# Order of VectorE's and ScalarE's work beside the projections of a first block: retention heads four pieces later, one square for eight exponentials

## The reference, cut to what matters

```python
xn = rms_norm(h, norm_in_g)
proj = xn @ w_in                       # 1024 x 6144
q, k, v, g_ret, x_lru, g_lru = split(proj)
q, k = rotary(q), rotary(k) * 128 ** -0.5          # 8 heads of 128
o_ret = group_norm_heads(chunkwise_retention(q, k, v))
y_ret = o_ret * silu(g_ret)

xc = causal_depthwise_conv(x_lru, conv_w, conv_b)
r = sigmoid(block_diag(xc, gate_a)); i = sigmoid(block_diag(xc, gate_x))
log_a = -8 * r * softplus(-lru_lambda)
a = exp(log_a)
mult = sqrt(max(1 - exp(2 * log_a), 0))
b = mult * (i * xc)
o_lru[t] = a[t] * o_lru[t - 1] + b[t]              # a scan over the tokens
y_lru = o_lru * silu(g_lru)
h = h + concat(y_ret, y_lru) @ w_out
```

## Time and profile before

| | us |
|---|---|
| median of 3 runs | 1706.65 (1706.38 to 1706.9) |
| the profiled execution | 1706.55 |
| its span | 1704.8 |
| TensorE busy | 1670.0 |
| VectorE busy | 1256.5 |
| ScalarE busy | 842.9 |

### The profile page before, as it was taken

The page is one execution under the profiler, slowest core; times in us unless marked ns, Lnnn a source line. Parts: engine busy times, 40 slices in busy tenths (PEclk is TensorE's granted clock), DMA queues, the critical chain, the costliest instruction groups (busy, mean ns, idle before and its releaser), DMA issues.

```text
span 1704.8 us, 25221 instructions
## 1 busy us (share of the span) xinstructions
PE 1670.0 (98%) x9808; PEld 1426.1 (84%) x9808; DVE 1256.5 (74%) x2205; ACT 842.9 (49%) x1370; POOL 0.2 (0%) x4
## 2 busy tenths in 40 slices
PE   9989999999999999999999999999999999999998
PEld 9888888777787778888888888889778989979997
DVE  7999777875778798856877775347756786678874
ACT  6665555554324443347444442336553455466653
POOL 0000000000000000000000000000000000000000
PEclk9999999999999999999999999999999999999999
DMA  8646543232234335533545556324322444547653
GB/s 340 228 161 236 193 152 108 67 123 62 69 111 161 121 133 186 206 128 99 141 149 188 191 196 222 99 75 139 101 83 64 134 147 152 172 156 169 196 198 124
DMA packets 79078, 254.91 MB, mean 150 GB/s; under 512 B 14320, under 2 KB 18672, under 8 KB 78320
## 3 DMA queue, kind: packets, MB, share of 16 engines
q1 hardware_dynamic: 73488, 244.91, 43.8%
q10 hardware_dynamic: 5472, 8.39, 1.5%
HBM read 252.19 MB, written 1.07 MB: 149 GB/s over the span
## 4 chain that ended last, share of the span: by engine, by line
PE 78%; DVE 13%; ACT 5%; issue 3%; DMA 0%; ACTq 0%; DVEq 0%
PE bank L725 66%; DVE w_lo L1830 3%; PE bank L868 2%; PE bank L1037 2%; PE bank L1023 2%; PE bank L1115 2%; PE bank L1014 2%; ACT w_hi L1225 1%; DVE mod_w L1887 1%; PE bank L1104 1%; DVE probT L1887 1%; DVE att L2460 1%; DVE xc L1930 1%; DVE resid_x L2326 0%; DVE bank L2458 0%
## 5 line engine op out<-in xcount | busy, mean ns | idle before, releaser
L1830 DVE TENSOR_TENSOR w_lo<-w_raw,w_hi 128x1024 fp32r<-128x1024 f32 (+1 forms) x356 | 426.9, 1210 | 253.5 <-ACT w_hi L1225 251.9
L1225 ACT ACTIVATE w_hi<-w_raw 128x1024 fp32r<-128x1024 f32 (+1 forms) x356 | 370.0, 1048 | 339.2 <-PE bank L725 284.5
L725 PE MATMUL bank<-hT_hi,w_hi 128*128 128x512 f32 (+1 forms) x1280 | 446.0, 348 | 1.7 <-ACT zo L1555 0.6
L725 PE MATMUL bank<-hT_hi,w_lo 128*128 128x512 f32 (+1 forms) x1280 | 437.5, 342 | 0.0
L725 PE MATMUL bank<-hT_lo,w_hi 128*128 128x512 f32 (+1 forms) x1280 | 437.3, 342 | 0.0
L725 PEld LDWEIGHTS bank<-hT_hi,w_hi 128*128 128x128 f32 x1280 | 242.2, 189 | 30.4 <-issue 3.1
L725 PEld LDWEIGHTS bank<-hT_hi,w_lo 128*128 128x128 f32 x1280 | 242.1, 189 | 27.9
L725 PEld LDWEIGHTS bank<-hT_lo,w_hi 128*128 128x128 f32 x1280 | 242.4, 189 | 27.1 <-issue 1.0
L1887 DVE SCALAR_TENSOR_TENSOR mod_w<-mod_w,c_rows 128x1024 f32<-128x1024 f32 x96 | 117.0, 1218 | 8.4 <-DMA mod_w<-in_mod_weights 8.4
L725 PE MATMUL bank<-w_hi,hT_hi 128*128 128x512 f32 x272 | 114.7, 422 | 0.4 <-issue 0.4
L725 PE MATMUL bank<-w_lo,hT_hi 128*128 128x512 f32 x272 | 106.6, 392 | 0.0
(11 more groups left out here) (393 smaller groups left out, 2794.9 us busy)
## 6 DMA issues: line engine op xcount, KB each, us to landing
w_raw<-in_weights SPq DMA_DIRECT2D x356, 512.0 KB, 3.9
mod_w<-in_mod_weights SPq DMA_DIRECT2D x96, 512.0 KB, 4.1
nbias<-in_window_bias ACTq DMA_DIRECT2D x32, 128.0 KB, 3.2
resid_c<-in_ctx ACTq DMA_DIRECT2D x2, 1024.0 KB, 6.8
gain_mix<-gain_rows SPq DMA_DIRECT2D x3, 512.0 KB, 5.7
gain_ffn<-gain_rows SPq DMA_DIRECT2D x3, 512.0 KB, 4.2
c_rows<-in_conditions SPq DMA_DIRECT2D x1, 1024.0 KB, 5.6
gatew<-in_gate_weights SPq DMA_DIRECT2D x1, 1024.0 KB, 11.6
```

The costliest lines, as they stand in the source:

```text
L725: mm = pe.matmul(held[key][:, oc], st, mv_, start=(opens and k == 0 and t == 0 and i == 0), stop=(closes and k == tiles - 1 and t == 2), s ...
L1225: a.activation(w_hi[:, p % RING, :, used], w_raw[:, p % RING, :].rearrange("p (k n) -> p k n", k=KP)[:, :, used], ACT.Copy).then_inc(hi_re ...
L1830: v.tensor_tensor(w_lo[:, p % RING, :, used], w_raw[:, p % RING, :].rearrange("p (k n) -> p k n", k=KP)[:, :, used], w_hi[:, p % RING, :, ...
```

## The change

The early retention heads start after skipping 8 products' banks, four pieces later, behind pieces 25, 27, ... 35. ScalarE writes a = exp(log_a) in place, and then the square of all of it in one instruction, in place of exp(2 log_a) by eight. VectorE's product by the square root is two halves (`lru_drive`), each scan waits for VectorE's instruction before it, and the decays, statistics, scans, gatings and lo halves stand in a new order, with the halves of the pieces placed explicitly and `ahead` reduced by 2 at decays and statistics. One modulation block moves ahead of head 7's product. ScalarE's order of square roots, silus and hi halves changes likewise.

```diff
+EARLY_SKIP = 8
-            early = Beside(retention_early(), RET_EVERY, 0)
+            early = Beside(retention_early(), RET_EVERY, EARLY_SKIP)
...
-            def ret_sqrt(h):
-                ahead(("ro", h))
+            def ret_sqrt(h, split=True):
+                if split:
+                    ahead(("ro", h))
...
             act.wait_ge(*lam_scaled.at(0))
+            act.wait_ge(*A.last())
             for n in range(HEADS):
-                act.wait_ge(*lru_ix.at(n))
-                a.activation(xc[:, n, :], lru_r[:, n, :], ACT.Exp, scale=lam[:, 1, n:n + 1]).then_inc(*A.tell(lru_e2, n))
+                a.activation(lru_r[:, n, :], lru_r[:, n, :], ACT.Exp, scale=lam[:, 0, n:n + 1]).then_inc(*A.tell(lru_a, n))
                 if n % 4 == 3:
                     split_hi(23 + n // 4)
             act.wait_ge(*A.last())
+            act.wait_ge(*lru_ix.at(HEADS - 1))
+            a.activation(xc[:], lru_r[:], ACT.Square).then_inc(*A.tell(lru_e2, 0))
             tok(4, v1, ACT.Copy)
-            for n in range(HEADS):
-                a.activation(lru_r[:, n, :], lru_r[:, n, :], ACT.Exp, scale=lam[:, 0, n:n + 1]).then_inc(*A.tell(lru_a, n))
-                if n % 4 == 3:
-                    split_hi(25 + n // 4)
+            split_hi(26)
             act.wait_ge(*lru_clamped.at(0))
             a.activation(xc[:], xc[:], ACT.Sqrt, bias=1.0).then_inc(*A.tell(lru_mult, 0))
             tok(5, sg, ACT.Silu)
```

VectorE:

```diff
+            def lru_drive(n):
+                v.tensor_tensor(lru_i[:, n:n + 4, :], lru_i[:, n:n + 4, :], xc[:, n:n + 4, :], ALU.mult).then_inc(*W.next())
             def lru_scan(n):
+                dve.wait_ge(*W.last())
...
-            for n in range(4, HEADS):
+            for n in range(4, HEADS - 1):
                 lru_input(n)
             mod_ops(2)
+            lru_input(HEADS - 1)
             split_lo(23)
             mod_ops(2)
-            dve.wait_ge(*lru_e2.at(HEADS - 1))
+            dve.wait_ge(*lru_e2.at(0))
             v.tensor_scalar(xc[:], xc[:], 1.0, -1.0, ALU.min, ALU.mult).then_inc(*W.tell(lru_clamped, 0))
             split_lo(24)
             mod_ops(2)
             split_lo(25)
             mod_ops(2)
             split_lo(26)
```

More of the change, by code:

```diff
@@ L1346, in _ @@
             tok(5, sg, ACT.Silu)
-            ret_sqrt(0)
-            ret_sqrt(1)
+            split_hi(30)
+            silu_T(6)
+            split_hi(32)
+            ret_sqrt(0, False)
+            split_hi(34)
+            ret_sqrt(1, False)
             ret_mix(0)
-            silu_T(6)
-            ret_sqrt(2)
+            split_hi(36)
+            ret_sqrt(2, False)
             ret_mix(1)
-            split_hi(32)
+            silu_T(7)
             for n in range(4):
                 lru_mix(n)
-            ret_sqrt(3)
+            split_hi(37)
+            ret_sqrt(3, False)
             ret_mix(2)
-            silu_T(7)
-            ret_mix(3)
-            split_hi(36)
             for n in range(4, HEADS):
                 lru_mix(n)
+            ret_mix(3)
             act.dma_start(gout_row[:], gout_in).then_inc(gout_loaded, 16)
@@ L1933, in conv_pair, with ret_decay @@
                     W.mark(conv_ready, n)
-            def ret_decay(h):
+            def ret_decay(h, more=0):
                 key = ("rs", h)
-                ahead(key)
+                ahead(key, more)
                 dve.wait_ge(*filled_at(key))
@@ L1944, in ret_decay, with ret_stats @@
                 v.tensor_tensor(sT[:, h % 2, T:T + P], ps[:, T:T + P], decay[:, h, 0:P], ALU.mult).then_inc(*W.drain(key))
-            def ret_stats(h):
+            def ret_stats(h, more=0):
                 key = ("ro", h)
-                ahead(key)
+                ahead(key, more)
                 dve.wait_ge(*filled_at(key))
@@ L1961, in ret_norm, with ret_var_of @@
                 ret_normed(h)
-            def ret_var_of(h):
-                ret_stats(h)
+            def ret_var_of(h, more=0):
+                ret_stats(h, more)
                 v.tensor_scalar(bnst[:, 2 + h % 2, 0:2], att[:, 2 * (h % 2):2 * (h % 2) + 2, 1], EPS, None, ALU.add)\
@@ L2058, in _ @@
             split_lo(26)
-            dve.wait_ge(decay_loaded, 16)
[L2060 to L2066, removed]
-                lru_scan(n)
+            dve.wait_ge(*lru_mult.at(0))
+            lru_drive(0)
+            split_lo(27)
+            lru_drive(4)
+            split_lo(28)
@@ L2068, in _ @@
+            dve.wait_ge(decay_loaded, 16)
+            ret_decay(0, -2)
+            for n in range(4):
+                lru_scan(n)
+            split_lo(29)
+            ret_decay(1, -2)
+            ret_var_of(0, -2)
+            split_lo(30)
+            ret_normed(0)
             for g in range(2):
-                ahead((("in", 5), g))
                 dve.wait_ge(*drained_at((("in", 5), g)))
             ret_gate(0)
-            ret_decay(2)
-            lru_scan(3)
-            ret_norm(1)
+            for n in (4, 5):
+                lru_scan(n)
@@ L2075, in _ @@
+            split_lo(31)
+            ret_decay(2, -2)
+            ret_var_of(1, -2)
+            lru_scan(6)
+            ret_normed(1)
             ret_gate(1)
+            split_lo(32)
             ret_lo(0)
[L2077 to L2080, removed]
+            lru_scan(7)
+            dve.wait_ge(*W.last())
+            for n in range(4):
+                lru_gating(n)
+            ret_decay(3, -2)
+            split_lo(34)
+            ret_var_of(2, -2)
@@ L2081, in _ @@
+            ret_normed(2)
             ret_gate(2)
             ret_lo(1)
[L2083 to L2086, removed]
+            for n in range(4, HEADS):
+                lru_gating(n)
+            split_lo(35)
+            ret_var_of(3, -2)
             for n in range(4):
-                lru_gating(n)
-            ret_norm(3)
+                lru_lo(n)
+            ret_normed(3)
             ret_gate(3)
             ret_lo(2)
-            for n in range(4):
-                lru_lo(n)
@@ L2094, in _ @@
-            split_lo(35)
-            ret_lo(3)
             split_lo(36)
             for n in range(4, HEADS):
-                lru_gating(n)
-            for n in range(4, HEADS):
                 lru_lo(n)
+            ret_lo(3)
             mod_ops(2)
```

## The result

The changed kernel takes 1710.18 us (median of 16 runs, 1709.62 to 1712.07) against 1706.71 for the kernel before on the same chips (16 runs, 1706.28 to 1707.56): 3.47 us more, ratio 1.002, 95% interval 1.0013 to 1.0027. The forecast was 1709.5, its range 1704 to 1712.3, and the likeliest case a loss. The profiled execution took 1709.74 us, span 1708.0.

The account below looks back on a forecast made before the run. VectorE's arrival at the second q block's rotation was taken to pace TensorE and the end: new idle 6.6 plus scans and drive 1.0 less old idle 4.7 gives +2.9 (2.85 by the walk), 1709.5 us, range 1704 to 1712.3.

Parts of the forecast that it names:

- the end follows VectorE's arrival at the rotation: A delay of VectorE at the second q block's rotation (line 1911, at 140.36 before) delays the end.
- The Square: ScalarE's one Square of 128x2048, 1.91 us, ends at 85.51; VectorE waits 4.6 us for it at the clamp.
- the case with one: A table load before the Square adds 1.28 us; chance 0.05, within a rival of 0.15 for late roots and loads.
- The 3.6 us wait and the clock behind it: TensorE's wait before the first retention output (line 800) and its half-speed clock go when retention starts four pieces later.
- The stalls at pieces 31 and 35: TensorE waits for VectorE's late lo halves, 1.5 us at piece 31 and 2.0 us at piece 35.
- The walk: VectorE's queue priced step by step from head 7's product to the second q block's rotation, reached at 143.2, 2.85 us later.
- the wait at piece 39: TensorE, there at 144.9, waits 3.6 us for VectorE's lo half, done at 148.5.
- counted 0 for the clock: Slow TensorE clock behind new gaps at pieces 23 and 39 adds 0, bounds 0 and 0.5 us.
- The term for the scans: VectorE's eight scans, each waiting for the instruction before, step 0.71 instead of 0.60: 0.9 us, bounds 0 and 1.0.
- the main case: The forecast of VectorE late at the rotation: +2.85 us, own range +1.2 to +4.5, chance 0.55.
- the terms for the scores of head 1: TensorE gives scores 1 only behind piece 27, at 104.95, leaving VectorE idle 1.06 us.
- a gain: Rival: retention no longer stalls TensorE and the Square is no wait; -3.7 up to -7.5 us, say 1701.5; chance 0.13.

Follow-up runs that it names:

- Experiments 2: Changed kernel with VectorE's second modulation pair and the lo half of piece 23 ahead of the wait for the Square: 1707.79 us, 0.56 over the kernel before.
- experiment 6: Changed kernel with one modulation block moved from ahead of the second q block's rotation to between lo halves of heads 5 and 6: 1707.99 us, 0.76 over kernel before.
- the kernel of four edits: Changed kernel with piece 23's work ahead of the Square wait, scans without waits, lo 35 earlier, one modulation block later: 1704.41 and 1704.28 us.
- experiment 4: Changed kernel with the lo half of piece 35 ahead of head 3's statistics instead of behind its gate: 1710.38 us, 3.15 over the kernel before.
- (1): Changed kernel with the square undone, eight Exp of the doubled exponent first as before: 1708.04 us, 0.81 over the kernel before.
- Experiment 5: Kernel before with the retention steps four pieces later and nothing else: 1712.9 us (5 runs), 6.0 over the kernel before.
- experiment 0: The changed kernel again, unaltered, on a second chip: 1710.25 us, 3.35 over the kernel before.
- (3): Changed kernel with the wait for VectorE's previous instruction kept at the first scan alone: 1710.16 us, 3.26 over the kernel before.
- experiment 8: The kernel of four edits with a second modulation block moved behind head 5's normalising and later loads for the last three blocks: 1703.08 us, ratio 0.9976.

## Why the prediction was right

**What bounds.** The claim that the end follows VectorE's arrival at the rotation is what the table shows, over a span of 10 us, within 0.6 us. Experiments 2 and 6 move nothing but VectorE's own work, and the time follows. That nothing is caught up later holds too: behind 200 us TensorE's listed waits are 16.9 to 17.3 us in all twelve traces. The sum of TensorE's waits up to 210 us goes roughly with the time, as it must where TensorE is the busiest engine, but misses it by up to 2.0 us: the kernel of four edits has 5.2 us of them in one execution and 6.8 in another, at the same distance and medians 0.13 us apart. It tells what was lost and not what to move; experiment 4 took one of these waits away and got it back.

**The square.** The Square was expected from 83.60 to 85.51 and ran from 83.57 to 85.47; VectorE's wait was to be 4.6 and was 4.59; TensorE's stall at piece 23 2.65 and was 2.64. That the wait is the main part of the loss is shown twice: with VectorE's input ready earlier (1) 2.5 to 2.7 us go, with the wait filled (2) 2.8 to 2.9. No table load came in front of it, so the case with one fell.

**The move and the new order.** The 3.6 us wait and the clock behind it went as forecast, and the time rose all the same. The stalls at pieces 31 and 35 were to be 1.5 and 2.0 and were 1.35 and 1.96. Experiment 5 adds what the prediction did not price: the move alone, under the old order, costs 6.0 us.

**What was off.** The rotation was forecast 2.85 us late and was 3.39 (3.47 by the distance). The walk ends at 143.21; less two modulation blocks of 2.29 it has the lo half of turned head 3 done at 138.63, and the trace has 138.97. That is a wait of 0.35 us for ScalarE's copy of turned head 3, which the sum left out: the clock fell to half behind the stall at piece 35, where I had not looked for it, and delayed the turning. The other 0.2 us are gaps in the two modulation blocks in a row, 4.78 us instead of 4.58. With the same slow clock the wait at piece 39 was 2.4 and not 3.6. In experiment 0, where the clock did not fall behind piece 35, it was 3.47, and the wait for turned head 3 is absent; there the clock fell at piece 23 instead, and the waits for scores were 2.1 in place of 1.7 us, the 0.4 us that the prediction named for that fall. I had counted 0 for the clock, and ahead of the rotation one fall with a price of about 0.4 us is there in either execution. The term for the scans had the right size, 0.9 us against 0.96 measured, and it belongs in the sum, since the idle times were walked with the longer steps. But it is not a cost that can be had back whole, as the lower end of the main case's range (+1.2) took it to be: taken out by themselves (3), the scans' waits moved the distance by 0.5 and the time by 0.1 us. A slip without effect: the terms for the scores of head 1 add to 104.89, not 104.95; the trace has 105.06.

**The chances.** The own range of the main case, 1707.9 to 1711.2, held it. Against a gain spoke that the Square can't end before 85.5, and the new order as it stands doesn't win that back. Another order does: experiment 6 leaves the wait for the Square at 4.6 us and wins 2.6 us behind it, and experiment 8 with the same Square is 4.1 us under the kernel before. The prediction weighed the given order only and says nothing of that.

## What to carry to other kernels

Where one engine feeds another in a fixed order, find the stretch in which the feeder is hardly ever idle and the fed engine waits for it, and price every edit by what it does to the feeder's arrival at the end of it; the fed engine's stalls only tell where the debt is called in. Before replacing several instructions by one that costs less, look at who waits for the first of their results: here the result of the cheaper square came 2.8 us later (85.47) than that of the exponentials (82.7). And work without a near reader, like the modulation blocks, is worth its full length when it is moved out of such a stretch, until the place where it lands has a reader of its own (2.6 us for the first block, 1.2 for the second).

## What was not expected of the hardware

The granted clock behind a wait of one length differs from execution to execution. Behind TensorE's wait of 2.64 us at piece 23 it stayed at 1.00 in the trace of the changed kernel and fell to 0.50 in that of experiment 0, for the same program; behind the wait of 1.96 us at piece 35 it was the other way round. The windows (length, busy times of the engines, granted clock, DMA share, GB/s), first of the changed kernel:

```profile
90.00:92.00 2.00, 1.59 (x10) 1.12 (x9) 2.00 (x4) 2.00 (x2) 0.00 (x0) 1.00 1.02 420
...
134.00:136.00 2.00, 2.00 (x12) 2.00 (x11) 2.00 (x7) 0.00 (x0) 0.00 (x0) 0.55 0.91 240
```

and of experiment 0:

```profile
90.00:92.00 2.00, 2.00 (x7) 1.52 (x6) 2.00 (x3) 1.99 (x2) 0.00 (x0) 0.50 0.76 305
...
136.00:138.00 2.00, 2.00 (x19) 2.00 (x18) 2.00 (x5) 0.00 (x0) 0.00 (x0) 1.00 0.92 342
```

The kernel of four edits has a second such pair behind its wait at piece 39, 2.97 us in the first trace and 2.98 in the second:

```profile
144.00:146.00 2.00, 1.89 (x9) 1.92 (x10) 2.00 (x3) 1.74 (x2) 0.00 (x0) 0.50 0.14 55
```
```profile
144.00:146.00 2.00, 2.00 (x19) 2.00 (x18) 2.00 (x5) 1.79 (x3) 0.00 (x0) 1.00 0.01 4
```

The other traces agree. Behind the wait of 2.6 us at piece 23 the clock fell in three of five traces (experiments 0, 4, 6), behind the one of 2.0 us at piece 35 in four of six (changed kernel, 1, 2, 6). The chip alone does not decide it: experiments 0 and 3 ran on one chip and are the same program up to piece 23, and only the first fell there. Behind the five waits of 3.47 us or more (before, 0, 3, 4, 5) it was at half each time.

The times don't tell the executions apart: the changed kernel's two medians are 3.5 and 3.4 us over the kernel before, those of the four edits 0.13 us apart. In this stretch TensorE has to wait for VectorE anyway, at piece 39 above all, and what the slow clock takes behind piece 35 that wait gives back: it is 2.40 us with it and 3.47 without. Why the clock falls in one execution and not in the other stays open.
